# Copying two tables into one in 256 pieces of 0.5 MB instead of 128 of 1 MB, with other limits on how many are in flight

## The reference

```python
def block(t):                                    # 128 tokens
    q = (t @ wq).reshape(PEER_BLOCK, PEER_HEADS, 2, PEER_DQ // 2)
    s = jnp.einsum('tpcd,pckd->tpck', q, sub_keys)
    ...                                          # top 16 of 16384 experts for each of 8 heads
    g = jax.nn.softmax(top, axis=-1)
    a = gelu(jnp.einsum('tpkd,td->tpk', u[idx], t))
    return jnp.einsum('tpk,tpkd->td', g * a, v[idx])
```

## Time and profile before

| | |
|---|---|
| median of 3 runs | 3428.85 us (3426.5 to 3430.01) |
| profiled execution, its own time | 3434.98 us |
| its span in the profile | 3433.2 us |
| PE / DVE / ACT / POOL busy | 2704.8 / 2001.0 / 1185.8 / 804.4 us |
| bytes moved by DMA | 848.26 MB, mean 247 GB/s |
| copies | 128 of 1024 KB, median 13.7 us (u) and 14.9 us (v) to landing |
| weight chunks | 304 of 512 KB, median 3.6 us to landing |

### The profile page before, as it was taken

How to read it: one execution, slowest core, us unless ns; L and a number is a source line. 1 busy time by engine, 2 the same in 40 slices (tenths; PEclk the granted TensorE clock), 3 DMA queues, 4 the chain that set the end, 5 groups by cost and what they waited for, 6 DMA issues and landing times.

```text
span 3433.2 us, 41220 instructions
## 1 busy us (share of the span) xinstructions
PE 2704.8 (79%) x15753; PEld 2245.6 (65%) x15753; DVE 2001.0 (58%) x3632; ACT 1185.8 (35%) x2151; POOL 804.4 (23%) x789
## 2 busy tenths in 40 slices
PE   4999857985555556556655679989999999899998
PEld 3887656774454545445544667677888777778886
DVE  2322545677776854784555555357875465678753
ACT  1111402245555555555556541242220102422201
POOL 0112520224444444454444422001000000110000
PEclk8999978997777787777687789989999999999999
DMA  8899997889999999999999962202332231023322
GB/s 275 270 298 307 321 321 201 260 298 372 421 421 421 421 421 421 421 413 421 421 420 419 421 257 92 68 1 92 97 93 91 80 117 56 1 92 98 93 91 80
DMA packets 155065, 848.26 MB, mean 247 GB/s; under 512 B 15440, under 2 KB 15696, under 8 KB 88208
## 3 DMA queue, kind: packets, MB, share of 16 engines
q0 software_dynamic: 109824, 680.83, 52.3%
q1 hardware_dynamic: 45072, 165.12, 14.4%
HBM read 841.70 MB, written 136.31 MB: 285 GB/s over the span
## 4 chain that ended last, share of the span: by engine, by line
PE 50%; DMA 31%; DVE 8%; ACT 5%; issue 3%; POOL 3%; ACTq 0%; SPq 0%; DVEq 0%; POOLq 0%
DMA AR<-peer_uv,XC 20%; PE PS L195 13%; PE PS L196 13%; PE PS L197 13%; DMA RHI_f<-peer_uv,XC 5%; DMA RING<-in_wstream 4%; DVE AR L1837 3%; POOL AR L561 2%; ACT HL L1448 1%; PE PS L704 1%; DMA peer_uv<-in_peer_v 1%; PE PS L934 1%; ACT AR L1448 1%; DVE RING_r L1628 1%; PE PS L1054 1%
## 5 line engine op out<-in xcount | busy, mean ns | idle before, releaser
L195 PE MATMUL PS<-AR_r,RHI 128*128 128x512 f32 (+2 forms) x1912 | 748.0, 391 | 24.5 <-DVE AR_r L1644 6.9
L934 PE MATMUL PS<-IDN,HL 128*128 128x128 f32 x2688 | 483.1, 350 | 339.6 <-ACT HL L1448 339.6
L197 PE MATMUL PS<-AR_r,RING_r 128*128 128x512 f32 (+2 forms) x1912 | 743.0, 389 | 0.0
L1837 DVE SCALAR_TENSOR_TENSOR AR<-AR 128x1024 f32<-128x1024 f32 x410 | 501.4, 1224 | 380.8 <-DMA AR<-peer_uv,XC 380.3
L934 PEld LDWEIGHTS PS<-IDN,HL 128*128 128x128 f32 x2688 | 419.3, 183 | 403.1 <-ACT HL L1448 395.9
L196 PE MATMUL PS<-AR_r,RHI 128*128 128x512 f32 (+1 forms) x1688 | 655.3, 388 | 0.0
L561 POOL DMA_INDIRECT AR<-peer_uv,XC x410 | 469.0, 1144 | 598.8 <-ACT HL L1448 315.8
L1626 DVE CAST RHI<-RING 128x1024 fp32r<-128x1024 f32 x256 | 179.0, 699 | 440.1 <-DMA RING<-in_wstream 437.8
L195 PEld LDWEIGHTS PS<-AR_r,RHI 128*128 128x128 f32 x1912 | 361.6, 189 | 102.8 <-issue 17.0
L197 PEld LDWEIGHTS PS<-AR_r,RING_r 128*128 128x128 f32 x1912 | 361.3, 189 | 74.2
L934 PE MATMUL PS<-IDN,AR 128*128 128x128 f32 x1408 | 247.8, 345 | 187.2 <-ACT AR L1448 187.2
(11 more groups left out here) (371 smaller groups left out, 3540.0 us busy)
## 6 DMA issues: line engine op xcount, KB each, us to landing
RING<-in_wstream SPq DMA_DIRECT2D x304, 512.0 KB, 3.6
peer_uv<-in_peer_u POOLq DMA_DIRECT2D x64, 1024.0 KB, 13.7
peer_uv<-in_peer_v POOLq DMA_DIRECT2D x64, 1024.0 KB, 14.9
AR<-peer_uv,XC POOLq DMA_INDIRECT x410, 14.3
XL<-in_xl SPq DMA_DIRECT2D x1, 2048.0 KB, 8.6
AR<-in_strips POOLq DMA_DIRECT2D x1, 2048.0 KB, 8.2
out_x<-XL SPq DMA_DIRECT2D x4, 512.0 KB, 2.7
AR<-in_na_bias POOLq DMA_DIRECT2D x1, 1536.0 KB, 6.9
```

The lines of the kernel that those rows point to most:

```text
L195: pe.matmul(out, sh, mh, start=start, stop=False)
L197: return pe.matmul(out, sl, mh, start=False, stop=stop)
L934: mm = pe.matmul(sum_bank(tt, k), scaled_row(n)[:, P * k:P * k + P], IDN[:], start=(j == 0 and k % 4 == 0), stop=(j == SLOTS - 1), is_tran ...
L1837: dve.scalar_tensor_tensor(u, u, 1.0, HT[:, n // SLOTS, :], ALU.mult, ALU.mult, accum_out=RAW[:, n:n + 1]).then_inc(dotted, 1)
```

## The change

A copy has 128 rows, 0.5 MiB, and there are 256. The pacing takes the number in flight as an argument and waits for the landing of the piece that many before. In mod1 GpSimd no longer stops at barrier 1: it announces phase 1 at once, waits until the first chunks have been used, issues 16 pieces with two in flight and 8 with three, and then waits for phase 1. In the projections it issues 106 pieces with four in flight, in the attention 44 (two ahead of 22 of the 32 bias tiles), then 4, and none between the context's level products. In the recurrence 12 pieces each wait for a count of used chunks as well (56, 58, ... 78), with two in flight; 16 with three in flight follow before phase 5 is waited for and phase 6 is announced. Then come 12, 4, 14 in `add_seven`, and the last 20 with three in flight.

```diff
-COPY_ROWS = 256
-COPIES, IN_FLIGHT = 2 * NKEYS * NKEYS // COPY_ROWS, 3
+COPY_ROWS = 128
+COPIES, IN_FLIGHT = 2 * NKEYS * NKEYS // COPY_ROWS, 4
...
-            def copies(n, paced=False):
+            def copies(n, in_flight=None, after_chunk=None):
                 for i in islice(to_copy, n):
-                    if paced:
-                        pool.wait_ge(uv_copied[i % IN_FLIGHT], 16 * (i // IN_FLIGHT))
+                    if in_flight is not None and i >= in_flight:
+                        a = i - in_flight
+                        pool.wait_ge(uv_copied[a % IN_FLIGHT], 16 * (a // IN_FLIGHT + 1))
+                    if after_chunk is not None:
+                        pool.wait_ge(chunk_used, next(after_chunk))
                     copy_rows(pool, i)
...
-            copies(9, paced=True)
-            barrier(pool, 1)
+            passing(pool, 1)
+            pool.wait_ge(chunk_used, 1)
+            copies(16, in_flight=2)
+            copies(8, in_flight=3)
+            pool.wait_ge(phase, 4 * 1)
             pool.dma_start(BT, t["na_bias"]).then_inc(s_bt, 16)
             passing(pool, 2)
-            copies(52, paced=True)
+            copies(106, in_flight=4)
...
-                if i % 4 != 3:
-                    copies(1)
+                if i % 16 not in (3, 6, 9, 12, 15):
+                    copies(2)
...
-            copies(2)
+            copies(4)
...
-                    if lv % 3 == 0:
-                        copies(1)
...
             passing(pool, 4)
             passing(pool, 5)
-            copies(14, paced=True)
+            copies(12, in_flight=2, after_chunk=iter(range(FIRST["mod2"] + 8, FIRST["mod3"] + 7, 2)))
+            copies(16, in_flight=3)
             pool.wait_ge(phase, 4 * 5)
             passing(pool, 6)
-            copies(6, paced=True)
+            copies(12, in_flight=3)
             pool.wait_ge(phase, 4 * 6)
...
-            copies(2)
-            add_seven(n2, "sq", SQUARES, behind=1)
+            copies(4)
+            add_seven(n2, "sq", SQUARES, behind=2)
             passing(pool, 7)
-            copies(COPIES, paced=True)
+            copies(COPIES, in_flight=3)
```

## The result

The changed kernel takes 3441.8 us (median of 9 runs, 3437.4 to 3453.1) where the kernel before took 3432.5 in the same session (9 runs, 3424.5 to 3440.8). The ratio of after to before is 1.0034, with a 95% interval of 1.0022 to 1.0047. It is slower, by 9.3 us in the medians and by 12 us in the ratio, not by the 27 that were forecast. The profiled execution happens to be the longest of the nine (3453.1, span 3451.3). The part of it behind the first gather is 2756.0 us against 2747.4, and among all the profiled executions of this study, whose code is the same there, that part varies between 2741 and 2758. So I judge by what comes ahead of the gather: it starts at 695.27 where it started at 685.75, 9.5 us later.

What follows compares the result with a forecast made beforehand. Copies were taken to set the first gather: second read-out pair at 568 - 3 - 12 = 553, plus 159.5, gives 712.5 instead of 685.75, +26.8 us passed on whole; median 3456, own range 3444 to 3474, with rivals 3434 to 3482.

Steps and rivals of the forecast that it cites:

- rival 3: First gather: TensorE and VectorE make up for a late first row, giving back up to 10 us; chance 0.13.
- The twelfth threshold: Recurrent stage: met only by the second read-out pair, so no copy is issued for some 40 us ahead of it.
- The stretch from the pair to the gather: Second read-out pair to first gather: remaining copies take 159.5 us including 9.5 us of idle, so the gather comes at 712.5.
- Start: Before barrier 1: first matmul at 15 us instead of 25.46, first barrier 11 us earlier (bounds 5 and 14).
- Recurrent stage: Recurrent stage: smaller backlog and paced release cut TensorE's waits for weight chunks, -12 us (bounds -5 and -19).
- Small pieces: All copies: half-size pieces with three in flight move at the same rate as before, 245 GB/s for paced copies.
- rival 1: Copies: half-size pieces move faster; at 400 GB/s alone 3410 us, at 325 near no change; chance 0.17, of which faster 0.10.
- First to second barrier: Between barriers 1 and 2: 53.5 MB at 228 GB/s, GpSimd 8 us late, 3 of the 11 us gained remain.
- the attention stage: Attention: two issues before a bias tile lie within GpSimd's waits, nothing for TensorE; 11 us if that cover were gone.
- a sign of being wrong: Copies alone: the prediction called itself wrong if they showed over 300 GB/s.
- rival 2: Copies: half-size pieces move slower or three in flight run dry; at 10% less +61 us, 3490; chance 0.2.

Runs made afterwards that it cites:

- release_two_earlier: Changed kernel with each of the twelve used-chunk thresholds lowered by two chunks (54 to 76); ratio to before 0.9916, median 3405.1 us.
- announce_first: Changed kernel with the 16 pieces behind the twelfth released one issued after phase 6 is announced; ratio to before 1.0019.
- start_only: Kernel before with only the changed start: barrier 1 announced and the first used chunks awaited ahead of its nine copies; ratio 0.9985.
- split_in_two: Kernel before with each 1 MiB copy issued as two transfers of 128 rows, in the order u, u, v, v; ratio 1.0021.
- six kernels named above the table: The changed kernel and five variants with the same program up to the level masks and through the attention; recurrent stage started between 397.4 and 404.7.
- split_alternate: Kernel before with each 1 MiB unit issued as halves of 128 rows alternating u, v, u, v, three units in flight; ratio to before 0.9934.
- split_far: Kernel before with half pieces alternating u, v, u, v, v's piece taken from and written to rows 8,192 away from u's; ratio 0.9922.
- split_quarter: Kernel before with each 1 MiB unit issued as four transfers of 64 rows, u, v, u, v, three units in flight; ratio 0.9921.
- tables_apart: Kernel before with its 1 MiB pieces in the old order, each table written without gaps into its half of the joined table; ratio 1.0199.
- apart_alternate: Kernel before with half pieces alternating u, v, u, v and each table written without gaps into its half of the joined table; ratio 0.9990.

## Why the prediction was off

The direction was right and the mechanism that it rests on as well; the size was 2 to 3 times too large (27 us for 9 to 12), and the mechanism was priced wrongly at two places. The measured 3441.8 lies inside the wide range and just below the forecast's own, which began at 3444.

**Right.** The gather's start is set by the copies and is passed on whole: 9.5 us of delay here against 9.3 in the median, 34.5 us of gain against 36.7 in the median in release_two_earlier. So rival 3 is out. The twelfth threshold is met only by the second read-out pair: 53 us without a copy, some 40 forecast. GpSimd's drain waits for its copies, GpSimd releases barrier 6, and that costs nothing in itself (announce_first). The stretch from the pair to the gather was forecast at 159.5 us and took 695.3 - 537.3 = 158.0. The number is right by two errors that cancel: paced copies ran at 296 to 298 GB/s instead of 245, but the DMA engines idled longer than the 9.5 us allowed. From 537.3 to 695.3 the queues took 87.7% of their time (70.0% for GpSimd's, 17.6% for SP's), which leaves about 19 us. The drain of barrier 7 is part of it: in its 18.2 us GpSimd issued no copy, and from 642 to 648 the engines had next to nothing to do (shares 0.21, 0.02 and 0.00 in three stretches of 2 us).

**Start.** First matmul 14.7, forecast 15; bias table 11 us earlier, forecast 11. With the old pieces the same start moved the bias table by 3.9 us only (start_only).

**The steps that failed** are two. The larger by its share of the miss is the term of "Recurrent stage", "-12 us (bounds -5 and -19)": it measured -25, and that is 13 of the 17.2 us by which the gather's start was missed. The other is "Small pieces": "So I take the same rate as before." It measured 259 GB/s instead of 228 between the first two barriers, which is 3.5 us, and may lie behind part of the first.

Small pieces: the argument looked at what a transfer costs by its size, and size indeed does nothing (split_in_two). But the change also halves the length of the turns between the two tables, and that is worth 19% of rate at equal bytes in flight (47.12 MB against 39.68), 11% in the changed kernel, which keeps fewer in flight (261 against 235 GB/s). I had written in rival 1 that the pattern of addresses or their order sets the rate, and then priced only the size. It enters between the first two barriers and, in part, in the recurrent term.

First to second barrier: 53.5 MB took 206.8 us, 259 GB/s, instead of 228; GpSimd was 17 us early where 8 late was forecast. The masks came at 320.8, 9.1 us earlier than before, forecast 3. Of this the attention stage, which was to cost nothing, gave back 2.6: the recurrent stage began at 401.7 (408.2 before), forecast 405.2. That is 3.5 us; the six kernels named above the table, alike up to here, began it between 397.4 and 404.7, so this term is known to within some 4 us.

The recurrent term: -12 us forecast, -25 measured (158.1 to 133.1), beyond the bound of -19. Of the 25, about 10 are fewer waits for chunks (9.0 against the 19.2 of the earlier trace rows, nearly the 12 forecast), and 10 are TensorE's own busy time. The other 5 are idle time whose end the profile puts down to nothing ("issue": 33.2 us before, 26.3 after, in the level steps), less some smaller waits that grew. Busy time by stretch, over the stage, before and after:

```profile
408.00:568.00 160.00, 101.48 (x2470) 94.06 (x2472) 67.69 (x101) 25.90 (x38) 45.08 (x57) 0.79 0.84 274
```

```profile
402.00:537.00 135.00, 91.31 (x2478) 85.18 (x2476) 70.61 (x100) 25.58 (x38) 44.49 (x47) 0.86 0.50 170
```

The same number of matmuls takes 91.3 us at a mean granted clock of 0.86 where it took 101.5 at 0.79. TensorE stood idle for 44 of 135 us where it had stood for 59 of 160, and the clock was granted at its level of 2.4 GHz, not 1.2, for more of the time. The forecast counted waits alone and left the clock out. Split_alternate, which changes only the order of the copies, shortens the stage by 13.0 us with as many bytes queued, outside the 8 us that I had allowed there; its waits for chunks are 18.1 us, hardly fewer, its busy time 96.0, at a clock of 0.82. Its siblings split_far and split_quarter shorten it by 7.4 and 20.7. So some of the 25 comes from the turns; that the rest comes from fewer copies in flight and in the level steps is likely but not shown. With a scatter of 7 us between kernels alike in this stage, I can't divide it further.

The sum: 3.5 and 13 us, less 0.8 by which GpSimd followed the second read-out pair later than assumed (537.3 - 534.8 = 2.5 us, where 568.0 - 566.3 = 1.7 was taken), bring its release to 537.3 where 553 was forecast. With the 1.5 us of the stretch behind it these are the 17.2 us by which 712.5 missed 695.3.

**Rival 1**, smaller pieces faster, was real in effect and wrong in name. At 296 to 298 alone it stayed below the 325 at which it was to end near no change, and just below the 300 that was to be a sign of being wrong. Of rival 2 the slower pieces did not appear. Three in flight do run a little dry, at DMA shares of 0.91 and 0.92 where the larger pieces had 1.01 and 1.02, and move more all the same.

## What to carry to other kernels

When a stream of copies sets the end, look for stretches in which its queue is empty before looking at its rate: one threshold that could only be met a stage later cost 36 us, and no barrier showed it as its own loss. Price the order of transfers separately from their size and number; here issuing two interleaved destinations in turns of 0.5 MiB instead of 1 gave 19% of rate for an edit of a few lines. When an engine's waits shrink, look also at its granted clock: here TensorE's busy time fell as much as its waits for chunks did. A wait of 30 us on the busiest engine is no loss where another stream ends later.

## What the runs showed of the hardware

Copies within HBM at an unchanged share of the engines (84.2%) moved 39.7 or 47.1 MB in 170 us by the order of their transfers alone: the busy share of the DMA doesn't tell the rate. A packet, 3.6 KB in the mean, took 210 ns in split_in_two and 177 in split_alternate.

Beside large packets the other queue starved. With 33 KB packets in GpSimd's queue (tables_apart) the weights' queue moved 6.26 MB in 170 us instead of 11.01, chunks landed after 41.5 us instead of 9.3, and GpSimd passed the second barrier at 408.1 instead of 329.9 us: the copies were faster (308 GB/s) and the kernel 2% slower. With 16 KB packets (apart_alternate) it moved 10.66 MB, and chunks landed after 17.0 us.

A drain on GpSimd lasted until its DMAs had landed and grew with what was queued: 10.6 us behind the bias table and copies, where the table landed 9.6 us after its issue, and 18.2 at barrier 7, behind pieces that took up to 22.5 us to land.
